# A two-block layer stack on one core: where remainders of weights are made, 512-column products in the second block, and the order of opening, norms and closing

## The chip, the cores and the metric

The kernel runs on one core of one Trainium2 chip. The metric is the device time of one execution in microseconds (us); lower is better. A core has TensorE (PE, the matrix engine; its weight loads are shown apart as PEld), VectorE (DVE), ScalarE (ACT), GpSimd (POOL) and SyncE (SP, which here only issues transfers). Each engine works through its own list of instructions in order and waits on semaphores of the others. All matrices are float32.

## The reference, cut to what matters

The input x is 256 tokens by 1024 features. Two blocks follow each other.

```python
# block 1
h = rms_norm(x, pre_mix_norm)
att_q, att_k, att_v, gdn_qkv, gdn_z, gdn_a, gdn_b = split(h @ w_in)
o_att = softmax attention, 8 heads of 64, causal, with a relative bias
o_gdn = gated delta rule: conv + silu, triangular solve per chunk, gated norm
x = x + rms_norm(concat(o_att, o_gdn) @ w_out, post_mix_norm)
h = rms_norm(x, pre_mlp_norm)
x = x + rms_norm(square(relu(h @ w_up)) @ w_down, post_mlp_norm)
# block 2
h = rmsnorm(x, g_mix)
xc, gb, gc, q, k, v, g_sw, gate_a, gate_r = split(h @ w_in_2)
y_a = (gb * conv3(gc * xc)) @ w_a_out_2          # 3 taps along the tokens
ret = two-way retention of rotary(q), rotary(k), v; 4 heads, decays from dec_f, dec_b
y_r = (normalized(ret) * silu(g_sw)) @ w_r_out_2
x = x + (sigmoid(gate_a) * y_a + sigmoid(gate_r) * y_r) @ w_o_2
h = rmsnorm(x, g_ffn)
x = x + (silu(h @ w_ff_gate_2) * (h @ w_ff_up_2)) @ w_ff_down_2
out = rmsnorm(x, g_final)
```

## The kernel before, in words

**Split products.** Every large product is made of three products of a 32-bit type that PE reads at full rate (fp32r). A value a is cut into a leading part ah (a cast) and a remainder al = a - ah, a weight w into wh and wl, and the product is wh*ah + wh*al + wl*ah.

**Units of weights.** The weights are streamed in 144 units of 1 MB (2048 numbers on each of 128 partitions; the first is half as large) in an order fixed by `plan()`. SP copies unit i into one of three slots of `raw`, once the remainder of unit i-3 is made. ACT makes the leading part `wh` (`hi`, line 1095), DVE the remainder `wl` (`lo`, line 1545), each in one of four slots. Both engines make unit i+2 where their list says `next_unit()` for unit i, between other work. PE may start a unit when its remainder is there. So a `lo` in DVE's list stands ahead of whatever comes behind it there, and each unit's arrival depends on where in the two lists `next_unit()` was written.

**Kinds of units.** `b_unit` (line 439) has the weights stationary and 256 tokens moving: 8 slices of k times 2 blocks of output columns times 3 products of 256 columns, all into one bank. `wide_unit` (lines 465 and 468) does the same unit with the leading part and the remainder of x side by side as one moving operand of 512 columns: 16 products of 512 columns with wh, 16 of 256 columns with wl, into two banks, whose right halves hold the sum of wh*al. Somebody must then add the halves: ACT copies the right halves out (line 1367 in the first MLP, 1512 and 1517 in the last) and DVE adds the left halves to the copy. `a_unit` (497) and `a_pair` (522) have activations stationary and 512 columns of weights moving, 24 products a unit. Only the two MLPs use `wide_unit`; the second block's 28 units for xc, gc, gb, the rotated q and k (`rot`) and g use `b_unit`.

**Banks.** The eight PSUM banks are 0 to 3, given out by name, and 4 to 7, given out in turn by `take`. `opened(b)` makes PE wait until the former content of bank b was read.

**Order of the stages** (us in the trace): opening, norm of x and transposes, 0 to 13; the projections of block 1 with the decay work, to 116; solving a triangular system in levels (line 728) with the eight heads of attention between its steps, to 154 (`att(n)` does the next n of 24 steps; `BESIDE` says how many go where); out projection with the delta rule's remaining small products (lines 779 to 866), to 200; `between("mlp")`, norms between mixer and MLP, to 215; first MLP, to 382; `between("mix2")`, to 397; in block 2 the groups i = 0..3 of xc, gc, gb with the convolution, to 467; rotations, `w_a_out`, scores and g, to 547; retention heads with g, gates and output products, to 750; the last MLP, to 935; closing norm, to 942.

**between.** DVE multiplies the product of token half t with its norm weights out of PSUM (`products`), ACT sums its squares, POOL takes the root (line 2130), DVE adds it to x (`post_half`), ACT sums the squares of x (`norm_x`), POOL again the root, both scale x (`scale_x`), PE transposes, ACT writes the leading parts (line 1145), DVE the remainders (line 1571), and PE runs two "C" units on them, once for each half t. The next unit's `hi` and `lo` come behind all that.

**The convolution's groups.** For each i, DVE makes uc = gc*xc, three taps for two halves, multiplies with gb, makes the remainder yl, and then two steps of the decay table `Dm` for head i. ACT makes the leading part yh and the exponential of `Dm`, and only then the next group's first `hi`; DVE's next `lo` waits for that.

## Time and profile before

| | us |
|---|---|
| median of 3 runs | 939.38 |
| the three runs | 939.35, 939.38, 943.61 |
| the profiled execution: its time | 943.77 |
| the profiled execution: first to last instruction | 942.0 |

| engine | busy, share of the span |
|---|---|
| PE | 97% |
| PEld | 85% |
| DVE | 62% |
| ACT | 47% |
| POOL | 9% |

The profiled execution's 943.77 us are its span of 942.0 and 1.8 us around it. The engines' rows tell when each was busy; what counts is what PE waited for, and at which clock it ran. The chain of waits is the list of what released what, followed back from the last instruction.

### The profile page before, as it was taken

What the parts mean: (1) busy time and instruction counts of PE and PEld (TensorE: products, weight loads), DVE (VectorE), ACT (ScalarE), POOL (GpSimd) and SP (SyncE); (2) the same over time, 40 slices, a digit from 0 to 9 for tenths busy, and PEclk for the clock granted to TensorE, in tenths of its full rate; (3) what the DMA queues carried; (4) which work ended last, traced back from release to release, by engine and by line L of the source; (5) the groups of instructions that cost most, each with busy time, mean ns of one, the idle gap of its engine ahead of it and who ended that gap; (6) DMA issues with size and microseconds to landing.
All of it is one profiled execution on the core that took longest, in us unless ns stands there. A gap on an engine that the chain in (4) does not pass through costs nothing.

```text
span 942.0 us, 13539 instructions
## 1 busy us (share of the span) xinstructions
PE 915.6 (97%) x5876; PEld 797.1 (85%) x5876; DVE 584.6 (62%) x671; ACT 446.5 (47%) x528; POOL 85.2 (9%) x92
## 2 busy tenths in 40 slices
PE   6999998999999999999999999999999999999996
PEld 5988887878888888799989988887888888888885
DVE  5689955467556656658674655545457657565554
ACT  5765364265444445654344244443444565454442
POOL 2033010010000000100032230101100000000000
PEclk9999997799999999999999999999999999999999
DMA  8635413215544455365564534454544445546431
GB/s 307 240 134 180 143 44 112 90 46 200 224 180 179 181 201 206 108 232 222 181 224 136 177 114 159 180 205 147 179 180 178 179 148 192 219 178 220 175 142 46
DMA packets 24220, 159.86 MB, mean 170 GB/s; under 512 B 3240, under 2 KB 3512, under 8 KB 5856
## 3 DMA queue, kind: packets, MB, share of 16 engines
q1 hardware_dynamic: 21600, 152.58, 44.5%
q0 software_dynamic: 2272, 6.24, 1.9%
q8 instruction: 46, 0.75, 0.3%
q10 hardware_dynamic: 288, 0.17, 0.1%
q14 instruction: 14, 0.11, 0.0%
HBM read 157.91 MB, written 2.63 MB: 170 GB/s over the span
## 4 chain that ended last, share of the span: by engine, by line
PE 87%; DVE 6%; ACT 4%; issue 2%; DMA 0%; POOL 0%; DVEq 0%; POOLq 0%; ACTq 0%
PE banks L497 32%; PE banks L439 22%; PE banks L465 13%; PE banks L468 7%; PE banks L522 3%; DVE t_wl L1545 2%; PE banks L418 2%; PE banks L728 2%; PE banks L975 1%; ACT t_wh L1095 1%; ACT t_hold L1114 1%; ACT t_hx L1145 1%; PE banks L926 1%; PE banks L1057 1%; DVE t_hx L1571 1%
## 5 line engine op out<-in xcount | busy, mean ns | idle before, releaser
L1545 DVE TENSOR_TENSOR t_wl<-t_raw,t_wh 128x2048 fp32r<-128x2048 f32 (+1 forms) x143 | 325.2, 2297 | 142.1 <-ACT t_wh L1095 140.5
L1095 ACT CAST t_wh<-t_raw 128x2048 fp32r<-128x2048 f32 (+1 forms) x143 | 267.0, 1898 | 35.3 <-PE banks L439 20.0
L439 PE MATMUL banks<-t_hx,t_wh 128*128 128x256 f32 x1232 | 225.2, 285 | 0.4 <-DVE t_wl L1545 0.4
L439 PEld LDWEIGHTS banks<-t_hx,t_wh 128*128 128x128 f32 x1232 | 193.8, 193 | 2.5 <-DVE t_wl L1545 0.8
L439 PE MATMUL banks<-t_hx,t_wl 128*128 128x256 f32 x616 | 175.0, 284 | 0.0
L465 PE MATMUL banks<-t_hx,t_wh 128*128 128x512 f32 x544 | 170.9, 396 | 0.4 <-DVE t_wl L1545 0.4
L468 PEld LDWEIGHTS banks<-t_hx,t_wl 128*128 128x128 f32 x544 | 102.2, 188 | 23.9
L439 PEld LDWEIGHTS banks<-t_hx,t_wl 128*128 128x128 f32 x616 | 119.0, 193 | 0.0
L468 PE MATMUL banks<-t_hx,t_wl 128*128 128x256 f32 x544 | 107.0, 278 | 0.0
L497 PE MATMUL banks<-t_wh,t_hx 128*128 128x512 f32 x320 | 103.9, 402 | 0.0
L465 PEld LDWEIGHTS banks<-t_hx,t_wh 128*128 128x128 f32 x544 | 84.5, 189 | 2.6 <-DVE t_wl L1545 0.8
L497 PEld LDWEIGHTS banks<-t_wh,t_hx 128*128 128x128 f32 x320 | 60.5, 191 | 13.1 <-issue 0.3
L497 PE MATMUL banks<-t_wl,t_hx 128*128 128x512 f32 x160 | 61.9, 396 | 0.0
L2130 POOL TENSOR_TENSOR t_st<-t_st,t_half 128x1 f32<-128x1 f32 (+1 forms) x18 | 10.6, 589 | 443.0 <-DVE t_st L1571 434.8
L497 PEld LDWEIGHTS banks<-t_wl,t_hx 128*128 128x128 f32 x160 | 30.6, 192 | 6.5 <-issue 0.2
L1367 ACT COPY t_tail<-banks 128x512 f32<-128x512 f32 x14 | 8.2, 586 | 57.8 <-PE banks L468 57.8
L497 PE MATMUL banks<-t_wh,t_mh 128*128 128x512 f32 x112 | 34.6, 390 | 0.0
L497 PE MATMUL banks<-t_wl,t_mh 128*128 128x512 f32 x112 | 34.5, 389 | 0.0
L497 PE MATMUL banks<-t_wh,t_ml 128*128 128x512 f32 x112 | 34.5, 389 | 0.0
L1563 DVE TENSOR_TENSOR t_rl<-banks,t_tail 128x512 f32<-128x512 f32 x14 | 9.7, 691 | 30.5 <-ACT t_tail L1367 30.4
L2225 POOL TENSOR_SCALAR t_gt<-t_gt,t_small 128x256 f32<-128x256 f32 x16 | 14.9, 942 | 111.7 <-ACT t_gt L1456 111.7
L497 PEld LDWEIGHTS banks<-t_wl,t_mh 128*128 128x128 f32 x112 | 21.0, 188 | 4.5
(296 smaller groups left out, 1217.1 us busy)
## 6 DMA issues: line engine op xcount, KB each, us to landing
t_raw<-in_W SPq DMA_DIRECT2D x143, 1024.0 KB, 4.9
skew<-scr POOLq DMA_DIRECT2D x1, 1536.0 KB, 17.2
t_x<-in_x SPq DMA_DIRECT2D x2, 512.0 KB, 4.8
t_T<-skew POOLq DMA_DIRECT2D x8, 128.0 KB, 2.4
out<-t_xt SPq DMA_DIRECT2D x4, 256.0 KB, 2.1
t_tab<-in_tab POOLq DMA_DIRECT2D x1, 640.0 KB, 6.1
t_raw<-in_W SPq DMA_DIRECT2D x1, 512.0 KB, 6.6
t_T<-skew POOLq DMA_DIRECT2D x8, 64.0 KB, 2.6
```

Source lines behind the costliest of these rows:

```text
L418: return e.transpose(o, i, ident[:])
L439: m = e.matmul(bank[b][:, c * S:c * S + S], W[w][:, h, k * 128 * nt + c * 128:k * 128 * nt + c * 128 + 128], H[a][:, k, :], start=first, s ...
L465: e.matmul(bank[b + c], M.wh[:, h, wk], M.hx[:, k, :, :].rearrange("p a s -> p (a s)"), start=k == 0, stop=False)
L468: m = e.matmul(bank[b + c][:, 0:S], M.wl[:, h, wk], M.hh[:, k, :], start=False, stop=k == 7)
L497: m = e.matmul(bank[outs[t][c]][:], act[a][:, ks[kk], t * 128:t * 128 + 128], W[w][:, h, kk * 512 * ncb + c * 512:kk * 512 * ncb + c * 512 ...
L522: m = e.matmul(bank[outs[t][c]][:], act[a][:, k, t * 128:t * 128 + 128], W[w][:, (i0 + u) % HR, kk * 1024 + c * 512:kk * 1024 + c * 512 + ...
L728: m = e.matmul(bank[b][p, i * 64:i * 64 + 64], left(p), right(p), start=True, stop=True)
L1095: e.copy(M.wh[:, h, 0:n], M.raw[:, r, 0:n]).then_inc(q.sem, q.tick(("hi", i)))
L1545: e.tensor_tensor(M.wl[:, h, 0:n], M.raw[:, r, 0:n], M.wh[:, h, 0:n].bitcast(F32), ALU.subtract).then_inc(q.sem, q.tick(("lo", i)))
L1563: return e.tensor_tensor(o, a, b, op).then_inc(q.sem, q.tick(*names))
L2130: return e.tensor_tensor(o, a, b, op).then_inc(q.sem, q.tick(*names))
L2225: e.tensor_scalar(M.gt[:, a, :], M.gt[:, a, :], gw[:, 4 * h + a:4 * h + a + 1], None, ALU.mult).then_inc(q.sem, q.tick(("gt", h, a)))
```

## The change

It does six things.

1. In attention, DVE's `next_unit()` that stood behind level 2's steps (a `lo`, line 1545) stands between the two groups of steps of level 1.
2. The 28 `b_unit`s of block 2 become `wide_unit`s. ACT copies the right halves into one of two slots of `M.rest` (`rest`), DVE adds the left halves (`whole`), and what read the bank reads the sum. gc and gb use banks 0 to 3; of the rotations, `rotate(h, 1)` goes ahead of `scores(h - 1)`.
3. The opening: PE starts with 14 products of `M.half` that nobody reads; the bias product goes to bank 0; unit 1 is made in halves (`hi_halves`, `lo_half`), and its product runs with k outside and starts at the first half.
4. `between`: the squares of half 1's first product are summed ahead of half 0's scaling, `post_half` and the sums of x's squares of half 1 go between the parts of half 0, and the unit that follows is made in halves.
5. The eight numbers of `log_decays` are made during the first MLP.
6. The closing multiplies x with g_final ahead of the root, and DVE scales 640 and ACT 384 columns with it.

```diff
--- before.py
+++ after.py
@@ -263,6 +263,7 @@
+    M.rest = M.wbc.rearrange("p (i n) -> p i n", i=2)
@@ -417,19 +418,21 @@
-            def b_unit(tile, arrived, by, name, kind="B", k_outer=False, mid=None):
+            def b_unit(tile, arrived, by, name, kind="B", k_outer=False, mid=None, halved=False):
...
-                q.wait_ge(DV, ("lo", i))
+                q.wait_ge(DV, ("lo", i, 0) if halved else ("lo", i))
...
+                    if k == 4 and halved:
+                        q.wait_ge(DV, ("lo", i))
...
@@ -584,8 +589,13 @@
+            q.wait_ge(PO, "half")
+            for i in range(14):
+                e.matmul(bank[7][:, 0:128], M.half[:], M.half[:], start=True, stop=True)
...
-            b = take("bias")
+            b = take("bias", 0)
@@ -609,7 +619,8 @@
-                b_unit(("conv", u), x_in, AC, ("cin", u), mid=queries_and_keys if u == 5 else None)
+                b_unit(("conv", u), x_in, AC, ("cin", u), k_outer=u == 0, halved=u == 0,
+                       mid=queries_and_keys if u == 5 else None)
@@ -909,15 +920,15 @@
-                b_unit(("xc", i), x_mix2, AC, ("gcv", i), k_outer=i == 0)
-                b_unit(("gc", i), x_mix2, DV, ("uc", i))
-                b_unit(("gb", i), x_mix2, DV, ("cvg", i))
+                wide_unit(("xc", i), x_mix2, DV, ("gcv", i))
+                wide_unit(("gc", i), x_mix2, DV, ("gcs0", i), pair=0)
+                wide_unit(("gb", i), x_mix2, DV, ("gbs0", i), pair=2)
...
-                b_unit(("rot", h, w), x_mix2, DV, ("rb", h, w))
+                wide_unit(("rot", h, w), x_mix2, DV, ("turned0", h, w))
...
-                b = take(("sc", h))
+                b = take(("sc", h), h)
@@ -930,9 +941,9 @@
+                rotate(h, 1)
...
-                rotate(h, 1)
...
@@ -964,9 +976,9 @@
-                    if h or u:
-                        b_unit(("g", h, u), x_mix2, AC, ("gts", h, u))
-                bs = [take(("rv", h, n)) for n in range(2)]
+                    if h:
+                        wide_unit(("g", h, u), x_mix2, DV, ("gsm", h, u))
+                bs = [take(("rv", h, n), None if h else n) for n in range(2)]
...
@@ -1148,22 +1161,25 @@
-                    if t:
+                    if (t, c) == (1, 1):
...
+                norm_x(g, 0)
+                squares(1, 0)
...
-                    norm_x(g, t)
...
-                        if t == 0 and k in (2, 4):
-                            squares(1, k // 2 - 1)
+                        if t == 0 and k == 2:
+                            squares(1, 1)
+                        if t == 0 and k >= 6:
+                            norm_half(g, 1, k - 6)
...
-                    if t == 1:
-                        hi(unit[0] + 3)
-                        unit[0] += 2
+                hi_halves()
+                hi(unit[0] + 3)
+                unit[0] += 2
@@ -1177,6 +1193,7 @@
+            hi_halves()
@@ -1382,6 +1399,11 @@
+                if i == 9:
+                    q.wait_ge(DV, "sp0")
+                    e.activation(M.sp, M.sp, ACT.Exp).then_inc(q.sem, q.tick("sp1"))
+                    q.wait_ge(q, "sp1")
+                    e.activation(M.sp, M.sp, ACT.Ln, bias=1.0).then_inc(q.sem, q.tick("sp2"))
@@ -1391,30 +1413,34 @@
...
+            rests = [0]
...
+            def rest(tile, seen):
...
+                s = rests[0] % 2
+                rests[0] += 1
+                q.wait_ge(PE, tile)
+                if seen:
+                    q.wait_ge(DV, seen)
+                e.copy(halves(M.rest[:, s, :]), both(M.banks, at[tile], 1)).then_inc(q.sem, q.tick((tile, "rest")))
...
-                q.wait_ge(PE, ("xc", i))
-                if i >= 2:
-                    q.wait_ge(DV, ("cyl", i - 2))
-                e.copy(M.gcv[:, i % 2], halves(bank[at["xc", i]][:])).then_inc(q.sem, q.tick(("gcv", i)))
-                next_unit()
-                next_unit()
+                rest(("xc", i), ("gcs", i - 1) if i else None)
+                next_unit()
+                rest(("gc", i), ("gbs", i - 1) if i else None)
+                next_unit()
+                rest(("gb", i), ("gcv", i))
...
-                if i == 0:
-                    log_decays()
...
-                next_unit()
+                rest(("rot", h, 0), ("turned", h - 1, 0) if h else ("gcs", 3))
+                next_unit()
+                rest(("rot", h, 1), ("turned", h - 1, 1) if h else ("gbs", 3))
...
@@ -1448,13 +1475,12 @@
-                    if h or u:
+                    if h:
...
-                    q.wait_ge(PE, ("g", h, u))
-                    if h:
-                        q.wait_ge(DV, ("rlo", h - 1, 1))
-                    e.activation(M.gt[:, 2 * u:2 * u + 2, :], halves(bank[at["g", h, u]][:]), ACT.Silu).then_inc(
-                        q.sem, q.tick(("gts", h, u)))
+                    rest(("g", h, u), ("gsm", h - 1, u) if h else ("turned", 3, u))
+                    gated = M.gt[:, 2 * u:2 * u + 2, :]
+                    q.wait_ge(DV, ("gsm", h, u))
+                    e.activation(gated, gated, ACT.Silu).then_inc(q.sem, q.tick(("gts", h, u)))
@@ -1526,6 +1552,10 @@
+                q.wait_ge(DV, ("xg", t, 0))
+                q.wait_ge(PO, ("rstd", "out", t))
+                e.activation(M.xt[:, t, 0:384], M.xt[:, t, 0:384], ACT.Copy, scale=M.ms[:, t:t + 1]).then_inc(
+                    q.sem, q.tick(("out", t)))
...
@@ -1612,29 +1642,34 @@
-            def post_half(g, t):
...
+            def post_half(g, t, c):
...
-                for t in range(2):
-                    post_half(g, t)
-                    norm_x(g, t)
-                    scale_x(g, t)
-                    if t == 0:
-                        products(g, 1, arrived)
-                        trailing_of_x(g, 0, range(0, 5), w)
-                        mean_square(g, 1)
-                        trailing_of_x(g, 0, range(5, 8), w)
-                    else:
-                        trailing_of_x(g, 1, range(8), w)
-                        lo(unit[0] + 3)
-                        unit[0] += 2
+                post_half(g, 0, 0)
+                post_half(g, 0, 1)
+                norm_x(g, 0)
+                scale_x(g, 0)
+                products(g, 1, arrived)
+                trailing_of_x(g, 0, range(0, 2), w)
+                mean_square(g, 1)
+                trailing_of_x(g, 0, range(2, 4), w)
+                post_half(g, 1, 0)
+                trailing_of_x(g, 0, range(4, 5), w)
+                post_half(g, 1, 1)
+                trailing_of_x(g, 0, range(5, 8), w)
+                norm_x(g, 1)
+                scale_x(g, 1)
+                trailing_of_x(g, 1, range(8), w)
+                lo_half(0)
+                lo_half(1)
+                lo(unit[0] + 3)
+                unit[0] += 2
@@ -1649,6 +1684,8 @@
+            lo_half(0)
+            lo_half(1)
@@ -1809,9 +1846,10 @@
-                att(sum(BESIDE[l]))
-                if l == 2:
+                att(BESIDE[l][0])
+                if l == 1:
...
+                att(BESIDE[l][1])
...
@@ -1902,6 +1941,15 @@
+                if i == 8:
+                    ts(M.lg, dec, -1.0, None, ALU.mult, None, "lg0")
+                    q.wait_ge(q, "lg0")
+                    stt(M.sp, M.lg, -1.0, M.lg, ALU.mult, ALU.min, "sp0")
+                elif i == 10:
+                    q.wait_ge(AC, "sp2")
+                    stt(M.sp, M.lg, 0.0, M.sp, ALU.max, ALU.add, "sp3")
+                    q.wait_ge(q, "sp3")
+                    ts(M.lg, M.sp, -1.0, None, ALU.mult, None, "lg")
@@ -1912,24 +1960,25 @@
...
+            rests = [0]
...
+            def whole(o, tile, name):
...
+                s = rests[0] % 2
+                rests[0] += 1
+                q.wait_ge(AC, (tile, "rest"))
+                tt(o, both(M.banks, at[tile], 0), halves(M.rest[:, s, :]), ALU.add, name)
...
-                next_unit()
-                q.wait_ge(PE, ("gc", i))
-                q.wait_ge(AC, ("gcv", i))
+                whole(M.gcv[:, s], ("xc", i), ("gcv", i))
+                next_unit()
+                v = halves(M.rest[:, rests[0] % 2, :])
+                whole(v, ("gc", i), ("gcs0", i))
+                q.wait_ge(q, ("gcs0", i))
...
-                tt(M.uc[:, s, :, 1:S + 1], halves(bank[at["gc", i]][:]), M.gcv[:, s], ALU.mult, ("uc", i))
+                tt(M.uc[:, s, :, 1:S + 1], v, M.gcv[:, s], ALU.mult, ("uc", i), ("gcs", i))
@@ -1943,14 +1992,14 @@
-                q.wait_ge(PE, ("gb", i))
+                v = halves(M.rest[:, rests[0] % 2, :])
+                whole(v, ("gb", i), ("gbs0", i))
+                q.wait_ge(q, ("gbs0", i))
...
-                tt(M.cv[:, s], M.cv[:, s], halves(bank[at["gb", i]][:]), ALU.mult, ("cvg", i))
+                tt(M.cv[:, s], M.cv[:, s], v, ALU.mult, ("cvg", i), ("gbs", i))
...
-                if i == 0:
-                    log_decays()
@@ -1959,15 +2008,16 @@
-                v = halves(bank[at["rot", h, w]][:])
-                q.wait_ge(PE, ("rot", h, w))
+                v = halves(M.rest[:, rests[0] % 2, :])
+                whole(v, ("rot", h, w), ("turned0", h, w))
+                q.wait_ge(q, ("turned0", h, w))
...
-                tt(halves(M.ra[:, w, 1, :]), v, rep(M.rope[:, 1, :], 2), ALU.mult, ("rb", h, w))
+                tt(halves(M.ra[:, w, 1, :]), v, rep(M.rope[:, 1, :], 2), ALU.mult, ("rb", h, w), ("turned", h, w))
...
@@ -2113,13 +2165,17 @@
-                add_back("out", "ff", t)
+                for c in range(2):
+                    d = M.x[:, t, cols(c)]
+                    q.wait_ge(PE, ("ff", t, c))
+                    tt(d, d, bank[2 * t + c][:], ALU.add, ("add", "out", t, c))
+                    q.wait_dma(LD["g_final"])
+                    q.wait_ge(q, ("add", "out", t, c))
+                    tt(M.xt[:, t, cols(c)], d, M.wbc[:, cols(c)], ALU.mult, ("xg", t, c))
...
-                for c in range(2):
-                    q.wait_ge(PO, ("rstd", "out", t))
-                    q.wait_dma(LD["g_final"])
-                    stt(M.xt[:, t, cols(c)], M.x[:, t, cols(c)], M.ms[:, t:t + 1], M.wbc[:, cols(c)], ALU.mult,
-                        ALU.mult, ("out", t, c))
+                q.wait_ge(PO, ("rstd", "out", t))
+                q.wait_ge(q, ("xg", t, 1))
+                ts(M.xt[:, t, 384:1024], M.xt[:, t, 384:1024], M.ms[:, t:t + 1], None, ALU.mult, None, ("out", t))
...
```

## Rows read from the trace of the kernel before

**Rows 1.** The page: busy us, share, instructions; granted clock in 40 slices, in tenths
```profile
PE 915.6 (97%) x5876; PEld 797.1 (85%) x5876; DVE 584.6 (62%) x671; ACT 446.5 (47%) x528; POOL 85.2 (9%) x92
...
PEclk9999997799999999999999999999999999999999
```
**Rows 2.** Windows: stretch, length, busy of PE, PEld, DVE, ACT, POOL, granted clock, DMA
```profile
14.00:16.00 2.00, 2.00 (x11) 2.00 (x11) 2.00 (x5) 2.00 (x2) 0.37 (x1) 0.50 1.02 431
...
149.80:152.50 2.70, 0.01 (x1) 0.01 (x1) 2.60 (x4) 0.58 (x1) 0.00 (x0) 1.00 0.00 0
...
153.85:174.33 20.48, 20.48 (x138) 17.10 (x140) 10.11 (x14) 5.35 (x6) 2.20 (x2) 0.50 0.46 170
```
**Rows 3.** The chain of waits, 149 to 178: start, us, what
```profile
149.58 2.20 DVE t_wl L1545
...
153.84 1.85 PE banks L789 x16
...
159.05 2.86 PE banks L497 x6
...
166.57 3.61 PE banks L840 x32
...
177.68 1.07 PE banks L789 x16
```
**Rows 4.** Timeline of attention: start, us, engine, line, operation [idle before]
```profile
138.67 0.56 DVE L1563 TENSOR_TENSOR t_P<-banks,t_T 128x384 f32<-128x384 f32 x1 [2.07 <-PE banks L660]
...
151.89 0.55 DVE L1567 TENSOR_SCALAR t_P<-t_P,t_gs 128x128 f32<-128x128 f32 x2
```
**Rows 5.** The chain of waits: first MLP, and block 2's units
```profile
233.05 5.45 PE banks L497 x24
244.06 5.45 PE banks L497 x24
...
507.50 11.51 PE banks L439 x96
```
**Rows 6.** DVE's timeline in the convolution's last group
```profile
466.75 0.69 DVE L1563 TENSOR_TENSOR t_cv<-t_cv,banks 128x512 f32<-128x512 f32 x1 [0.63 <-PE banks L439]
468.12 0.69 DVE L1563 TENSOR_TENSOR t_yl<-t_cv,t_yh 128x512 fp32r<-128x512 f32 x1 [0.69 <-ACT t_yh L1409]
...
472.56 2.29 DVE L1545 TENSOR_TENSOR t_wl<-t_raw,t_wh 128x2048 fp32r<-128x2048 f32 x1 [2.56 <-ACT t_wh L1095]
```
**Rows 7.** Windows: the convolution's last group, from one such lo to the next
```profile
455.28:472.56 17.28, 17.28 (x147) 17.28 (x146) 12.21 (x14) 7.30 (x7) 0.00 (x0) 1.00 0.51 183
```
**Rows 8.** Timeline of the first MLP: the copy of the right halves and the sum
```profile
244.10 0.59 ACT L1367 COPY t_tail<-banks 128x512 f32<-128x512 f32 x1 [4.62 <-PE banks L468]
...
244.78 0.69 DVE L1563 TENSOR_TENSOR t_rl<-banks,t_tail 128x512 f32<-128x512 f32 x1 [2.53 <-ACT t_tail L1367]
```
**Rows 9.** Timeline between the blocks
```profile
386.19 1.41 DVE L1571 SCALAR_TENSOR_TENSOR t_x<-t_xt,t_st,t_x 128x512 f32<-128x512 f32 x2
389.36 0.49 DVE L1567 TENSOR_SCALAR t_xt<-t_x,t_st 128x512 f32<-128x512 f32 x1 [0.66 <-POOL t_st L2130]
...
394.99 4.49 DVE L1545 TENSOR_TENSOR t_wl<-t_raw,t_wh 128x2048 fp32r<-128x2048 f32 x2 [1.51 <-ACT t_wh L1095]
...
397.34 0.50 PE L439 MATMUL banks<-t_hx,t_wh 128*128 128x256 f32 x2 [0.42 <-DVE t_wl L1545]
```
**Rows 10.** Timeline of the opening
```profile
11.66 3.22 DVE L1571 SCALAR_TENSOR_TENSOR t_hx<-banks,t_small,t_hx 128x256 fp32r<-128x256 f32 x8
...
12.59 0.81 PE L592 MATMUL banks<-t_cout 32*8 32x384 f32 x2 [1.63 <-DVE t_hx L1571]
...
15.27 4.47 DVE L1545 TENSOR_TENSOR t_wl<-t_raw,t_wh 128x2048 fp32r<-128x2048 f32 x2
```
**Rows 11.** Timeline of the closing
```profile
935.80 0.69 DVE L1563 TENSOR_TENSOR t_x<-t_x,banks 128x512 f32<-128x512 f32 x1 [0.67 <-PE banks L522]
...
938.09 1.41 DVE L1571 SCALAR_TENSOR_TENSOR t_xt<-t_x,t_st,t_hold 128x512 f32<-128x512 f32 x2 [0.66 <-POOL t_st L2130]
```

55 lines of the change are left out of this document (23 added, 32 removed).

## The prediction, made before the changed kernel ran

> **What bounds the kernel now.** I read the page's busy times first: PE is busy 97% of the span and no other engine over 62% [rows 1]. So time can go only where PE is idle, where it runs on a low clock, or where its own products get cheaper. The windows come next, for the granted clock. It is full nearly everywhere, but from 153.85 to 174.33 us it is 0.50 (1.2 instead of 2.4 GHz) while PE is busy for all 20.48 us, and it is 0.50 once more behind the opening [rows 2]. Ahead of the long stretch PE was idle for 2.70 us, from 149.80 to 152.50 [rows 2]. The chain of waits says why: DVE's remainder of a weight unit (line 1545) runs from 149.58 to 151.78, and behind it in DVE's list stands the norm of attention's last head, from 151.89, which PE's next transposes wait for [rows 3, 4]. The reader should see there that an instruction of 2.2 us which nobody needs at that moment stands between two that somebody waits for, and that the stretch at half clock begins right behind the idle it makes.
>
> **Attention (edit 1).** The idle goes from 2.70 us to about 0.5: once its last remainder of attention's output is made at 149.58, DVE goes straight to the norm, whose two scalings (0.55) and the small reciprocal ahead of them end at 150.25 [rows 3, 4]. That is 2.2 us. The moved remainder lands behind DVE's work for head 4 or so, at about 136.6, and ends at about 138.9. The addition that stands behind it starts at 138.67 today after an idle time of 2.07 us [rows 4], so it is late by some 0.2 us and PE's next transposes are a level further on: cost 0. If that cover were gone it would cost at most the 2.2 us again. The unit's slot of raw data comes free 13 us sooner, so one transfer moves to a time in which DMA was idle; no price.
>
> What follows if PE's idle stays at 0.5 us is the larger part. I expect the clock not to fall, since between the opening and 153.85 it stayed at 2.4 GHz [rows 1] through all of attention's shorter waits, and fell behind the one of 2.70. Then 20.48 us of busy PE run at twice the clock. Two kinds of work stand in the chain at either level: the 16 products of line 789 took 1.85 us at half and 1.07 at full clock, a factor of 1.73; six products of line 497 took 2.86 at half, and 24 take 5.45 at full, so six take 1.36, a factor of 2.1 [rows 3, 5]. The stretch therefore shrinks to between 9.8 and 11.8 us: a gain of 8.6 to 10.7. I take 9.8, as the line-840 products (3.61 us) [rows 3] and the other small ones lie between. What is late next: DVE's and ACT's copies of 0.6 to 0.7 us between the triangular solve's products, which half clock covered. I count 0.2 us for them, with 2 as the far end. Sum for attention: 2.2 + 9.8 - 0.2 = 11.8 us (range 7 to 12.9 with the clock up).
>
> **Wide units in block 2 (edit 2).** A `b_unit` takes 11.51/2 = 5.755 us, 48 products at 120 ns. In the first MLP one period is 244.06 - 233.05 = 11.01 us, of which 5.45 are the 24 products of line 497, so a `wide_unit` takes 5.56 [rows 5]. The 28 units save 28 x 0.19 = 5.4 us. The moving columns are the same in number: 512 + 256 against 3 x 256. What is saved is a fixed part of some 12 ns for each product left out. The Trainium skill (TensorE: Matmul & The Clock Gate, Back-to-back issue gap) gives an isolated gap of N/2.4 + 2.5 ns, by which one 512-column product instead of two of 256 saves 2.6 ns and the 28 units about 1.2 us as an estimate; the rows' 120 ns speak against it, and the sum goes by them.
>
> Each of these units now costs ACT a copy of 0.59 us and DVE a sum of 0.69 [rows 8], and 28 of each lie in engines that are not the bound. The exception is the convolution. There DVE, ACT and DVE form a ring: DVE's work of one group, then ACT's exponential and its cast of the next unit (DVE idle 2.56 us), then DVE again. One turn today is 12.21 us of DVE's work, 2.56 for that and 0.69 in which DVE waits for ACT's yh: 15.5 us [rows 6, 7], against PE's 3 x 5.755 = 17.3. The change adds 3 x 0.69 us and a few hundredths for each wait of DVE on itself: 17.6 to 17.8. PE's three units shrink to 16.7. So the ring, not PE, sets the pace at an excess of about 1 us a group. Its reserve: the remainder that starts at 472.56 is ready at 474.8, and its unit is due when PE has done two more units after the last gb, which ended by 466.7: at 478.2. That is 3.4 us, of which the copy and sum of gb take 1.3 and the shorter units 0.4, which leaves 1.7. Four turns use up 4 and PE waits about 2 us in all (0 to 4.5). log_decays' removal from the first group (edit 5) gives that turn some 2 us back, but the first turn has PE behind the norms anyway; I count 0, and 0 for its work in the first MLP, whose ACT and DVE are idle 4.6 and 2.5 us a unit there [rows 8]. The rotations, scores and g units have far less DVE work per unit; their longer path (copy, sum, then what read the bank) of 1.3 us is covered by at least one more unit of PE, 5.5 us. Cost 0; with the cover gone, 1.3 us for each of 16. Net of edits 2 and 5: 5.4 - 2.0 = 3.4 us (0.9 to 5.4).
>
> **Between (edit 4), twice.** Half 1's path today is: `post_half` begins at 386.19, its two parts of 0.7, ACT's two sums, the root, the scaling at 389.36, transposes, then ACT's cast and DVE's remainder from 394.99, and PE's next unit at 397.34, released by that remainder [rows 9]. With the parts set between half 0's remainders, the second addition ends about 0.9 us sooner, and the path is then held by ACT, which has two sums and two leading parts to do in turn: scaling at about 388.4. The cast and remainder in halves overlap: half a cast (1.0) and half a remainder (1.2) are no longer in line, so the unit is ready 0.8 us sooner again. PE's own "C" unit then ends at about the same moment (24 products, 5.45 us, after half 1's first remainder). I take 1.6 us for each `between`, 3.2 in all (2 to 4).
>
> **Opening (edit 3).** The first unit starts at 13.4 today, behind a bias product of 0.81 us that itself waited 1.63 us for a bank which DVE was reading [rows 10]. With bank 0 it waits for nothing and leaves the line. The first unit is then paced by DVE's eight remainders of x (3.22 us from 11.66, so up to 14.88) and ends at 15.3 to 16.5, by the clock. The next starts at 17.8 today; with `lo_half(0)` behind the remainders (14.9 + 1.2) it starts at 16.1 to 16.5. The half clock seen at 14 to 16 us [rows 2] may stay, and then takes some 0.5 back. I take 1.2 us (0.3 to 1.9). The 14 products that nobody reads run while PE has nothing else until 7.0; even at half clock they end about then: 0, or 0.3 against.
>
> **Closing (edit 6).** Behind the last root DVE has two products of 0.7 us, 1.41 from 938.09 [rows 11]. Now ACT and DVE each do one part at once, about 0.6 us, and the multiplication with g_final falls into DVE's idle time around 935.80. The last transfer starts 0.8 us sooner but is larger (320 KB against 256 KB) and runs beside the other. I take 0.5 (0 to 0.8).
>
> **Sum.** 11.8 + 3.4 + 3.2 + 1.2 + 0.5 = 20.1 us off the profiled execution's 943.8 (span 942.0 and 1.8 around it): 923.7 us. That execution is 4.4 us above the median; one of the three timed runs is as high (943.61), two are at 939.4. What differs between them isn't in one trace. The length of the stretch at half clock is the likeliest, and since that is to go, I measure from the profiled execution and expect 15.7 us (1.7%) against the median. If the 4.4 us are something else, the new median is 919.3.
>
> **Rivals.** First, the clock falls all the same. For it: attention's last steps and the solve are small products with small gaps, and it fell once in the opening with PE partly busy. Against: it held through 130 us of the same kind of work. Then only the idle of 2.2 us goes and the other edits' 8.3: 943.8 - 10.5 = 933.3 us. Second, the ring in the convolution and the longer path in the other groups cost more, 5 us beyond the sum: 928.7. Third, the 4.4 us lie elsewhere: 919.3. Fourth, slower: each time PE waits for the ring in the convolution the clock falls as it did behind the 2.70 us, and a stretch like the one seen (20.48 us, 9.8 lost) follows. It decides from two such falls on, which take back the whole gain against the median; with four groups and three falls it is 923.7 + 29 = 953. Against it: the expected waits are about 1 us each and waits of that size left the clock alone elsewhere. The Trainium skill (TensorE: Matmul & The Clock Gate, A second HAM failure mode: psum-queue depth-cycling) tells of a kernel of 512-column products in which short idle times between groups made the clock swing between its two levels; the first MLP, which has such products, shows no swing here, so I give the rival little. Fifth, the edits in attention don't shorten anything, since something else holds PE at 150 as long: 935.
>
> **How the numbers follow.** The forecast has a chance of 0.62, the first rival 0.12, the second 0.1, the third 0.1, slower 0.03, the fifth 0.03. The range from 918.0 to 931.5 us holds the forecast with its bounds, the second and the third; the first (933.3) is left out. Against 939.4, a difference under 0.5% (4.7 us) is about what a measurement of this kernel can't tell from none, so faster begins at 934.7: the forecast, the first three rivals but for some of the first, 0.92. Same, between 934.7 and 944.1: 0.05. Slower 0.03.
>
> **What would show it.** Right: no window of half clock near 150 to 175, PE's idle there under 1 us, the part from 149.8 to the out projection's last group 12 us shorter; the wide units at 5.56 us; waits of PE on line 1545 of 1 us each in the third or fourth group of the convolution; PE's first unit behind each `between` 1.6 us sooner. Wrong: a granted clock of 0.50 over ten or more us, PE idle on DVE or ACT in the rotations or in the heads, or a `between` as long as before because ACT's sums come later than the transposes.

## The result, and the profile after

The changed kernel takes 927.82 us (median of 4 executions, 924.72 to 928.88) against 939.37 for the kernel before beside it (938.82 to 943.61, 4 executions): ratio 0.986, 95% interval 0.983 to 0.990. The prediction was 923.7 us with a range of 918.0 to 931.5. So the direction was right and the time lies in the range, 4.1 us above the forecast: of the 15.7 us that were expected against the median of before, 11.6 were measured.

The page of the changed kernel shows what [rows 1] showed of before: busy us and share of each engine, then the granted clock in 40 slices.

```profile
PE 906.8 (98%) x5456; PEld 770.2 (83%) x5456; DVE 603.7 (65%) x704; ACT 461.4 (50%) x557; POOL 91.1 (10%) x92
...
PEclk9999999999999999999999999999999999999999
```

PE has 420 products fewer and is busy 8.8 us less, and the slices at 0.7 in attention are gone. The windows (length, busy time of PE, PEld, DVE, ACT and POOL, granted clock, DMA) answer to [rows 2]:

```profile
12.30:15.70 3.40, 3.18 (x15) 3.21 (x16) 3.40 (x8) 3.40 (x6) 0.00 (x0) 0.51 1.02 424
32.70:36.10 3.40, 3.40 (x19) 3.40 (x19) 2.42 (x2) 3.35 (x5) 0.14 (x1) 0.52 0.31 127
150.00:175.00 25.00, 24.07 (x262) 19.20 (x259) 14.50 (x20) 11.62 (x17) 2.21 (x2) 1.00 0.29 106
```

The long stretch at 1.2 GHz is gone. The one in the opening (12.30 to 15.70) is there still, and there is a second one behind it, which before did not have. The chain of waits of the changed kernel (start, length, what), cut to one line for each place that the change touches:

```profile
17.75 7.14 DMA scr<-t_cout
...
32.94 13.10 PE banks L442 x96
...
120.49 2.01 PE banks L739 x64
...
152.69 0.56 DVE t_P L1597 x2
...
153.30 0.55 PE banks L419 x3
...
180.27 4.10 PE banks L527 x18
...
387.23 0.70 PE banks L470 x2
...
465.86 22.08 PE banks L502 x96
```

Read against [rows 3]: the norm of the last head (DVE, two scalings, 0.56) and PE's transposes now follow one another with no remainder of 2.2 us ahead of them, and PE's wait for that norm (us in total, times, longest) is 0.5 where it was 2.7:

```profile
PE banks L419 <- DVE t_P L1597: 0.5, 1, 0.5
```

The opening, though, has a transfer in its chain for 7.14 us which in before was nowhere in the chain. Marks that both kernels pass at the same point of their work turn this into a table (start of the mark in us from the span's start, profiled executions; the last column is the difference that the part itself adds):

| mark | before | after | part | its share |
|---|---|---|---|---|
| first products of the triangular solve (x64) | 117.48 | 120.49 | opening, edit 3 | +3.0 |
| out projection's pair of units (x18) | 188.00 | 180.27 | attention, edit 1 | -10.7 |
| first MLP's first output products (x24) | 222.02 | 213.01 | first place between blocks, edit 4 | -1.3 |
| first MLP's last ones behind a wide unit (x24) | 354.19 | 345.18 | first MLP | 0.0 |
| first unit of block 2 | 397.34 | 387.23 | second place between blocks, edit 4 | -1.1 |
| products of `w_a_out` behind the convolution (x96) | 478.23 | 465.86 | convolution, edits 2 and 5 | -2.3 |
| first rv products (x8) | 552.97 | 539.42 | rotations and scores | -1.2 |
| last MLP, start | 751.41 | 736.69 | heads | -1.2 |
| last MLP, near its end | 907.17 | 892.42 | last MLP | 0.0 |
| end of the span | 942.0 | 927.1 | closing, edit 6 | -0.1 |

The sum is 14.9 us between two profiled executions, where 20.1 were forecast. The 5.2 missing are mostly the opening (+3.0 instead of -1.2), and attention, which gave 10.7 instead of 11.8. The profiled execution of the changed kernel (928.88) is the slowest of its four, 1.1 above their median, and the experiments show that its opening is the worst one seen. So this table explains the profiled execution; the opening of a median execution need not have lost as much.

### The profile page after: what moved, and what is told of

Read it like the earlier page. It is cut to its first block, busy times and chain, and to the rows that moved or that the text cites. A ratio compares the mean times of both kernels' runs of the same rounds, so it can differ in the third digit from the quotient of the medians.

```text
span 927.1 us, 12760 instructions
## 1 busy us (share of the span) xinstructions
PE 906.8 (98%) x5456; PEld 770.2 (83%) x5456; DVE 603.7 (65%) x704; ACT 461.4 (50%) x557; POOL 91.1 (10%) x92
## 4 chain that ended last, share of the span: by engine, by line
PE 79%; DVE 11%; ACT 6%; issue 2%; DMA 1%; POOL 1%; POOLq 0%; DVEq 0%; ACTq 0%
PE banks L502 32%; PE banks L470 20%; PE banks L473 10%; DVE t_wl L1575 4%; PE banks L442 4%; ACT t_wh L1107 2%; PE banks L527 2%; PE banks L739 2%; PE banks L419 2%; PE banks L987 1%; PE banks L582 1%; DMA scr<-t_cout 1%; DVE t_hx L1601 1%; PE banks L937 1%; PE banks L1069 1%
## 5 line engine op out<-in xcount | busy, mean ns | idle before, releaser
L1575 DVE TENSOR_TENSOR t_wl<-t_raw,t_wh 128x2048 fp32r<-128x2048 f32 (+1 forms) x140 | 319.2, 2302 | 125.9 <-ACT t_wh L1107 124.7
L470 PE MATMUL banks<-t_hx,t_wh 128*128 128x512 f32 x992 | 312.2, 396 | 1.0 <-ACT t_vv L1185 0.5
L1107 ACT CAST t_wh<-t_raw 128x2048 fp32r<-128x2048 f32 (+1 forms) x140 | 262.5, 1899 | 13.1 <-DMA t_raw<-in_W 7.6
L473 PE MATMUL banks<-t_hx,t_wl 128*128 128x256 f32 x992 | 194.9, 278 | 0.0
L470 PEld LDWEIGHTS banks<-t_hx,t_wh 128*128 128x128 f32 x992 | 153.2, 189 | 4.0 <-DVE t_wl L1589 1.8
L502 PE MATMUL banks<-t_wh,t_hx 128*128 128x512 f32 x320 | 102.0, 395 | 0.0
L442 PE MATMUL banks<-t_hx,t_wh 128*128 128x256 f32 x336 | 64.2, 293 | 1.5 <-DVE t_hx L1601 1.5
L442 PEld LDWEIGHTS banks<-t_hx,t_wh 128*128 128x128 f32 x336 | 54.8, 201 | 2.6 <-DVE t_hx L1601 2.2
L1425 ACT COPY t_hold<-banks 128x512 f32<-128x512 f32 x28 | 16.4, 585 | 68.6 <-PE banks L473 57.5
L442 PE MATMUL banks<-t_hx,t_wl 128*128 128x256 f32 x168 | 48.8, 290 | 0.0
```

Source lines behind the costliest of these rows:

```text
L442: m = e.matmul(bank[b][:, c * S:c * S + S], W[w][:, h, k * 128 * nt + c * 128:k * 128 * nt + c * 128 + 128], H[a][:, k, :], start=first, s ...
L470: e.matmul(bank[b + c], M.wh[:, h, wk], M.hx[:, k, :, :].rearrange("p a s -> p (a s)"), start=k == 0, stop=False)
L473: m = e.matmul(bank[b + c][:, 0:S], M.wl[:, h, wk], M.hh[:, k, :], start=False, stop=k == 7)
L502: m = e.matmul(bank[outs[t][c]][:], act[a][:, ks[kk], t * 128:t * 128 + 128], W[w][:, h, kk * 512 * ncb + c * 512:kk * 512 * ncb + c * 512 ...
L1107: e.copy(M.wh[:, h, 0:n], M.raw[:, r, 0:n]).then_inc(q.sem, q.tick(("hi", i)))
L1425: e.copy(halves(M.rest[:, s, :]), both(M.banks, at[tile], 1)).then_inc(q.sem, q.tick((tile, "rest")))
```

## Experiments

Three questions were open. Is the gain in attention the idle time or the clock, and does the one always cause the other? What does the opening lose, and where? What do wide units, their ring and the two places between the blocks cost by themselves? "Before beside it" is the kernel before on the same chip in the same session.

**The opening: bias row first.** DVE makes the relative bias row ahead of the halves of the first remainder, as before had it; all else is the changed kernel.

```diff
-            lo_half(0)
-            lo_half(1)
             q.wait_ge(PE, "bias")
             q.wait_dma(LD["neg"])
             tt(M.rrow, bank[at["bias"]][0:8, 0:384], M.ng, ALU.add, "row")
+            lo_half(0)
+            lo_half(1)
```

> Theory (transfer queued behind weights): in the changed kernel the 12 KB row for the attention bias is ready on DVE only after the two halves of the first remainders, its transfer is issued at 17.75 us, behind a weight transfer that the second half released at 16.9, and takes 7.1 us instead of 1.8; ACT's first tap and so PE's 'sums' product wait for it. Here DVE makes the row ahead of the two halves and nothing else is changed. The transfer should be issued at about 15.8, land by 18 us, PE's wait of 3.5 us on line 1601 should fall to the 0.5 of the kernel before, no window of half clock near 33 to 36 us: 3 to 5 us less than the changed kernel's 927.8, so 923 to 925, 0.982 to 0.985 of the kernel before. Rival (the opening is late for another reason, such as the 14 products or DVE's extra halves): the transfer lands early but the 3 us at 46 us stay: 927 to 928.

**The opening: nobody waits for the transfer.** The order of the changed kernel stays, but ACT waits for the row's transfer only from its third part on, and POOL clears the pad ahead of it.

```diff
-                q.wait_dma(LD["scr"])
+                if u == 2:
+                    q.wait_dma(LD["scr"])
...
+            e.memset(M.cin[:, :, 0:3], 0.0).then_inc(q.sem, q.tick("pad"))
             q.wait_ge(DV, "row")
...
-            e.memset(M.cin[:, :, 0:3], 0.0).then_inc(q.sem, q.tick("pad"))
```

> Same theory, from the other side: the order on DVE stays that of the changed kernel and the transfer stays slow, but nobody waits for it where it hurts. ACT waits for it only from the third convolution unit on (the first whose output lies over the row), and POOL clears the padding ahead of it. Expected as above: PE's wait of 3.5 us gone though the transfer still takes about 7 us, 923 to 925 us. If instead it is the place of the row among DVE's work that costs, this run stays at 927 to 928 and only the run with the row first is faster.

Measured: 926.21 us (926.01 to 928.09, 4 executions, ratio 0.984, 0.979 to 0.989) with the row first and 926.01 (924.44 to 928.18, ratio 0.984, 0.979 to 0.988) without the wait. Both were expected at 923 to 925 and missed that. They are 1.6 and 1.8 below the changed kernel's median, not the 4.3 that the opening of its profiled execution lost; in both profiles some of it went again in attention, where the clock fell near 160 us (table below). The DMA view from 12 to 30 us (out<-in, queue, operation, KB, median us from issue to landing) of the kernel before, of the changed one, and of the one with the row first:

```profile
scr<-t_cout POOLq DMA_DIRECT2D x1, 12.0 KB, 1.8
```
```profile
scr<-t_cout POOLq DMA_DIRECT2D x1, 12.0 KB, 7.1
```
```profile
scr<-t_cout POOLq DMA_DIRECT2D x1, 12.0 KB, 2.0
```

What waited for it, in the changed kernel: POOL's timeline, one line of ACT's, and the waits of PE (us in total, times, longest).

```profile
17.75 0.53 POOL L2216 DMA_DIRECT2D scr<-t_cout  x1 [8.53 <-DVE t_cout L1593]
25.16 1.11 POOL L2218 DMA_DIRECT2D skew<-scr  x1 [6.89 <-DMA scr<-t_cout]
26.26 0.15 POOL L2219 MEMSET t_cin<- 128x36 f32 x1
...
26.50 0.91 ACT L1233 ACTIVATE t_cout<-t_cin,t_small 128x256 f32<-128x256 f32 x2 [3.04 <-POOL t_cin L2219]
...
PE banks L636 <- DVE t_gs L1601: 3.5, 1, 3.5
```

With the row first that wait of PE is 0.5, and without ACT's wait it is 0.5 too:

```profile
PE banks L636 <- DVE t_gs L1601: 0.5, 1, 0.5
```

The first products of the solve come at 116.21 and 116.46 instead of 120.49. Both cures work, by separate ways, so the path is shown: the row was made 2.1 us later (16.91 instead of 14.80), its transfer of 12 KB started at 17.75 instead of 15.6, and there it took 7.1 us instead of 1.8. In the seven other profiles with the late start it took 4.3 to 6.2 us, in the six with the early start 1.8 to 2.0.

What lies between the two starts can be seen in the DMA's columns (the last two: busy share of the DMA engines, GB/s), first in before, then in the changed kernel:

```profile
17.00:18.00 1.00, 1.00 (x9) 1.00 (x9) 1.00 (x2) 0.00 (x0) 0.24 (x1) 0.84 0.00 0
```
```profile
18.00:24.89 6.89, 6.89 (x60) 6.89 (x59) 3.85 (x2) 1.90 (x2) 0.27 (x1) 1.00 0.96 356
```

In all profiles the engines are all but idle from 17 to 18 us, and then the next weights of 1024 KB come, which SP issued at 17.0 to 17.6. The early transfer lands ahead of them. The late one is issued behind them: in the changed kernel SP issues at 17.02, POOL at 17.75, and POOL's queue moves no packet before 21 us. Why it takes 7.1 us in one execution and 4.3 in another stays open.

How much this costs differs as much. In the six other profiles that have both the late row and ACT's wait for its transfer, PE waits 0.7 to 2.2 us instead of 3.5, and the solve's first products come at 116.52 to 118.50, against 116.21 with the row first and 117.48 in before. So the profiled execution of the changed kernel is the worst of seven: there the moved row cost 4.3 us, in the others 0.3 to 2.3, and in four of these six the opening is still 0.5 to 1.0 us shorter than in before. PE's wait of 3.5 us is also followed by the second stretch at half clock (32.7 to 36.1), which no profile with a wait of 2.2 us or less shows there. With the row first the opening gains 1.3 us over before, where 1.2 were forecast.

**Attention alone.** The kernel before with edit 1 and nothing else:

```diff
-                att(sum(BESIDE[l]))
-                if l == 2:
+                att(BESIDE[l][0])
+                if l == 1:
                     next_unit()
+                att(BESIDE[l][1])
```

> The kernel before with edit 1 alone (DVE's remainder moved between the steps of attention's level 1). Theory: PE's idle of 2.7 us ahead of the last head's transposes goes to 0.5 and the stretch at half clock behind it goes too; in the profile, 10 to 12 us less between 145 and 175 us than in the kernel before. Against the median of the kernel before 7 to 11 us less (928 to 932), depending on how long that kernel's typical stretch at half clock is. Rival (the clock falls for another reason, such as the small products themselves): a stretch at 0.50 in this profile too, and only 2.2 us less, 937.

**The kernel before again**, unchanged, for a second profile:

> The kernel before unchanged, for a second look. Theory for the 4.4 us between its executions: a fast execution (939.4) has a shorter stretch at half clock behind 150 us than the 20.5 us of the one profiled, by some 8 to 9 us, or starts its opening differently. If this profile falls at 943 too, its stretch should be about as long as the first. Rival: a time of 939 with the same 20.5 us at half clock, and the difference elsewhere.

**Attention undone.** The changed kernel with that edit taken back, the same lines the other way round:

> The changed kernel with edit 1 undone, in three rounds. Theory: PE's idle of 2.7 us is back, 2.2 us are always lost, and in some executions the clock falls behind it for long, as in the kernel before, whose 14 executions lie at 937 to 939 and at 944 to 945 us. So two groups of times here too: about 928 to 930, and 934 to 937. Rival (the long fall comes from the kernel's other small products and not from this idle time): all executions within 2 us of the changed kernel's 927.8 + 2.2.

Measured: attention alone 935.01 us (934.32 to 936.30, 10 executions) against a median of 943.5 for before beside it (936.77 to 944.99, 13 executions), ratio 0.993 (0.991 to 0.996). Before again 936.88. Attention undone 931.93 (931.06 to 936.66, 10 executions), ratio 0.993 (0.990 to 0.996). Attention alone missed its 928 to 932; between profiles the part from the solve to the out projection got 9.3 us shorter (70.5 to 61.2), where 10 to 12 were expected. Attention undone has two groups, as expected, the lower one 1 to 2 us later than expected. The second profile of the kernel before is the telling one. Its chain, and its windows at the place where [rows 2] had 0.50:

```profile
151.22 2.20 DVE t_wl L1545
...
154.14 0.55 PE banks L418 x3
...
149.50:154.10 4.60, 1.94 (x37) 1.47 (x36) 3.25 (x5) 1.55 (x4) 0.00 (x0) 1.00 0.00 0
153.80:174.30 20.50, 19.73 (x200) 15.86 (x201) 12.86 (x18) 8.62 (x9) 2.20 (x2) 1.00 0.54 181
```

The same remainder of 2.20 us stands in the same place, PE is idle for the same 2.7 us (4.60 less 1.94), and the clock does not fall. In the changed kernel with edit 1 undone it does fall, for as long as in [rows 2]:

```profile
153.40:173.90 20.50, 20.50 (x140) 17.11 (x141) 10.25 (x14) 5.29 (x6) 2.20 (x2) 0.50 0.47 169
```

and with edit 1 alone there is a short fall further on, behind PE's waits at the end of the solve:

```profile
161.10:164.50 3.40, 3.40 (x18) 2.30 (x17) 1.76 (x5) 0.00 (x0) 1.51 (x1) 0.50 0.97 330
```

From the solve's first products (x64) to the out projection's pair (x18), with attention's last heads between, the profiles give, by PE's idle time ahead of the last head and by the time at half clock from 150 to 175 us:

| kernel profiled | idle, us | half clock, us | length, us |
|---|---|---|---|
| before | 2.7 | 20.5 | 70.5 |
| attention undone | 2.7 | 20.5 | 70.5 |
| before again | 2.7 | 0 | 62.0 |
| no wait for the transfer | 0.5 | 6.8 | 62.9 |
| attention alone, row first, narrow units | 0.5 | 3.4 | 61.2, 61.3, 61.3 |
| after, and three variants of it | 0.5 | 0 | 59.8, each |
| remainder later | none to 0.5 | 0 | 59.2 |

That splits the gain of 10.7 without a model: 62.0 - 59.8 = 2.2 us are the idle time; 70.5 - 62.0 = 8.5 us are the clock, which go only where it falls for as long. And it shows that the fall isn't settled by the kernel: with the same idle time one execution has it and another has not. The times of the kernel before say the same. Of its 48 executions beside the experiments 30 took 935.0 to 939.6 us and 18 took 943.5 to 945.1, with nothing between; the upper ones have a mean clock of 0.986 to 0.988, the lower ones 0.992 to 0.998. With edit 1 alone ten of ten lie under 936.4. With edit 1 undone four of ten lie at 936.2 to 936.7 and six at 931.1 to 932.3. So edit 1 takes away the upper group, and taking edit 1 back brings it again: that the long fall hangs on the remainder's place, and the idle time that it makes, is shown both ways.

The distance between the groups' medians is 5.8 us (944.6 and 938.8), though, and not 8.5. The second profile of before, at 936.88, is one of the six fastest of the 30 (up to 936.9, mean clock 0.996 to 0.998); the other 24 take 937.5 to 939.6 at 0.992 to 0.995. So the usual executions of before show more time at half clock than those six, and with edit 1 undone the lower six, at 0.991 to 0.992, more still. None of these was profiled, and where their clock falls is not shown; part of it can lie in the opening. It fits that attention alone is 3.8 us under the median of the lower group, more than the 2.2 of the idle time.

The Trainium skill (TensorE: Matmul & The Clock Gate, What's actually happening) says that half rate is the default state which activity lifts, and that the moment at which the chip judges activity isn't tied to the start of the kernel, so that executions of one kernel differ. The traces agree: here one and the same 2.7 us of idle time was followed by a fall that cost 8.5 us in two profiles, and by none in a third.

**Narrow units.** The changed kernel with edits 2 and 5 undone: block 2 in `b_unit`s of three times 256 columns.

```diff
-                wide_unit(("xc", i), x_mix2, DV, ("gcv", i))
-                wide_unit(("gc", i), x_mix2, DV, ("gcs0", i), pair=0)
-                wide_unit(("gb", i), x_mix2, DV, ("gbs0", i), pair=2)
+                b_unit(("xc", i), x_mix2, AC, ("gcv", i), k_outer=i == 0)
+                b_unit(("gc", i), x_mix2, DV, ("uc", i))
+                b_unit(("gb", i), x_mix2, DV, ("cvg", i))
```

> The changed kernel with edits 2 and 5 undone: block 2's 28 units are narrow again (three products of 256 columns) and the decays' logarithms are made in the convolution. Read by stage in the trace: from the first unit behind the second 'between' to the first w_a_out unit 80.9 us as in the kernel before (78.6 in the changed one), and to the last MLP's first line-502 unit 4.6 us more than the changed kernel. Rival (the gain of block 2 came from the moved logarithms or from less waiting, not from the width): the 14 units of the convolution and first rotations take under 80 us here too.

**The ring.** The changed kernel, with ACT's cast of the next unit ahead of its copy of `gb` and of the exponential's part behind it:

```diff
                 next_unit()
+                hi(unit[0] + AHEAD)
                 rest(("gb", i), ("gcv", i))
```

> The changed kernel, with ACT's cast for the next group's third unit ahead made while PE still works on gb, so that DVE's next remainder no longer waits for ACT's exponential and cast. Theory (the ring of DVE and ACT sets the pace of the convolution's groups, 17.3 us a turn against 16.7 of PE): DVE's idle of 2.56 us ahead of that remainder vanishes, and the stretch from the first wide unit to w_a_out falls from 78.6 to 77.9 us, no more, since PE's reserve had covered nearly all of the ring. Rival (the ring had cost the 2 us that were forecast): 76.6 or less.

Measured: narrow 931.14 us, ring 924.44 (one execution each). From block 2's "C" units to the end of the span, narrow units take 557.6 us (371.80 to 929.4), the changed kernel 553.0 (374.12 to 927.1), the ring's variant 552.3 (370.33 to 922.6). So edits 2 and 5 gain 4.6 us, and 5.3 with the ring loosened; without any ring 5.4 were forecast. The rival of the narrow kernel (the gain came from the moved logarithms or from less waiting) is out: its 14 units take 80.86 us, as before had it (80.89), with the changed kernel's 78.63 beside them:

```profile
384.91 80.86 PE banks L441 x672
```

The chain of the changed kernel shows the ring at work, one remainder of DVE to the next of the following group:

```profile
402.92 2.20 DVE t_wl L1575
...
420.23 2.20 DVE t_wl L1575
...
437.55 2.20 DVE t_wl L1575
...
454.86 2.20 DVE t_wl L1575
```

One turn is 17.3 us, not the 17.6 to 17.8 of the forecast. The windows of the third turn, to set beside [rows 7]:

```profile
437.55:454.86 17.31, 17.31 (x101) 15.09 (x100) 13.92 (x18) 8.75 (x9) 0.00 (x0) 1.00 0.52 184
```

DVE is busy for 13.92 us of it, 1.71 more than in [rows 7], where three sums of 0.69 had been forecast as 2.07. PE's idle time from it is one wait at the end of the convolution, in the waits of PE:

```profile
PE banks L502 <- DVE t_wl L1575: 0.3, 1, 0.3
```

With the ring's cast moved that line is gone, the convolution is 0.4 us shorter, and the output products behind it (x96) take 21.79 instead of 22.08. The ring cost 0.7 us where 2.0 were forecast, 0.4 of it in the convolution itself, where 0.7 had been expected.

**Copies first, between the blocks.** In both places ACT's two copies that empty the first units' banks go ahead of its cast of the next unit.

```diff
-                hi(unit[0] + 3)
-                unit[0] += 2
                 for t in range(2):
                     q.wait_ge(PE, ("first", g, t))
                     e.copy(dst[:, t, :], bank[at["first", g, t]][:]).then_inc(q.sem, q.tick(taken(t)))
+                hi(unit[0] + 3)
+                unit[0] += 2
```

> The changed kernel with ACT's two copies of the 'C' units' products ahead of the cast of the unit after the next, in both stretches between the blocks. Theory (with the bias product off the rotation of the banks, the first wide unit gets the bank of the first 'C' product, which ACT reads only behind a cast of 1.8 us): PE's two waits of 0.5 us on line 1185 go, each wide unit starts 0.5 us sooner, 1.0 us in all by stage. Rival (PE then waits for the remainder, line 1589, instead): under 0.3 us in all.

Measured: 926.69 us (one execution). The changed kernel has two waits that before did not have, one in each place:

```profile
PE banks L470 <- ACT t_vv L1185: 0.5, 1, 0.5
PE banks L470 <- ACT t_up L1185: 0.5, 1, 0.5
```

Both are gone with the copies first, but in the first place another one comes for them:

```profile
PE banks L502 <- DVE t_ml L1593: 1.3, 1, 1.3
```

There ACT's cast, now later, holds DVE's remainder, and behind that in DVE's list stands the first MLP's square. From the first place's "C" unit to the second's it takes 181.8 us instead of 180.9 (190.69 to 372.53, 193.22 to 374.12); from there to the output products behind the convolution 91.1 instead of 91.7. So the order gains 0.6 in the second place and loses 0.9 in the first, where 1.0 in all was expected.

**No warm products.** The changed kernel without the 14 products that nobody reads.

```diff
-            q.wait_ge(PO, "half")
-            for i in range(14):
-                e.matmul(bank[7][:, 0:128], M.half[:], M.half[:], start=True, stop=True)
```

> The changed kernel without the 14 products that nobody reads. Theory (they gain nothing, since the first units wait for x and for DVE): the first unit of the convolution ends within 0.3 us of the changed kernel's, the transposes take longer but end before anyone waits for them, and one stretch of half clock lies in the first 20 us as before. Rival (they hold the clock up): transposes at twice the length and the first two units 1 us or more later.

Measured: 924.87 us (one execution). The granted clock of that kernel reads 1.00 in the opening:

```profile
12.00:16.00 4.00, 3.97 (x18) 3.32 (x17) 4.00 (x10) 4.00 (x7) 0.00 (x0) 1.00 1.02 424
```

But the products don't bear that out. PE's timeline has the first eight transposes and two pairs of the first unit's products, all of one shape; below them are the transposes of the changed kernel:

```profile
7.07 1.97 PE L419 MATMUL banks<-t_ident,t_xt 128*128 128x128 f32 x8 [7.07 <-DVE t_xt L1594]
...
15.40 0.62 PE L442 MATMUL banks<-t_hx,t_wh 128*128 128x256 f32 x2
...
15.98 0.40 PE L442 MATMUL banks<-t_hx,t_wh 128*128 128x256 f32 x2
```
```profile
6.88 1.09 PE L419 MATMUL banks<-t_ident,t_xt 128*128 128x128 f32 x8 [0.34 <-DVE t_xt L1597]
```

A pair takes 0.62 us up to 15.8, as the pairs at a granted clock of 0.50 do in before (0.63), and 0.40 behind it. So here PE worked at half clock from its first product until 15.8 us, and the value of 1.00 ahead of that doesn't tell its clock. The second profile of before is another such case: its pairs take 0.63 until 19.6 us, at a shown clock of 1.00. Read by their products, all 14 profiles have half clock in the first unit of weights. It ends at 15.8 to 18.7 us in the ten with the 14 products and at 15.9, 17.3, 17.7 and 19.8 in the four without.

So the 14 products did raise the clock for the transposes (1.09 us instead of 1.97), but it fell again at 11.5 to 14.2 us, ahead of the first unit or in its first products, and the first unit started only 0.2 us sooner (12.52 instead of 12.71). Without them the solve's first products come at 116.52, no later than in any of the six profiles that differ in that (116.68 to 120.49 with the same late row and wait). They gained nothing that can be seen here, as expected.

**Remainder later.** In the changed kernel DVE's remainder of the next unit, which stood between two of attention's last steps (160.28 in the chain), goes behind the delta rule's residual `r1` (t_cin), which PE waits for.

```diff
-            next_unit()
             att(len(STEPS) - taken[0])
...
                     tt(M.r1, M.tm[:, 1, 1024:1536], M.r1, ALU.subtract, "r1")
+            next_unit()
```

> The changed kernel with DVE's next remainder moved behind the copies of the state's products. In the changed kernel and in two of its variants PE waits 0.42 us at about 159 to 163 us for a copy that stands behind that remainder (2.3 us) on DVE, and in three of four profiles a stretch of 3.4 to 6.8 us at half clock begins there. Theory (that wait starts the fall): the wait goes, no stretch at 0.50 near 160, 0.4 us plus up to 3 us less, 924 to 927. Rival (the products there are sparse enough to let the clock fall with no wait at all): the wait is gone and the stretch is there in some executions; the times spread over 3 us as before.

Measured: 925.75 us (925.13 to 926.50, 4 executions), ratio 0.984 (0.979 to 0.989). The part from the solve's first products to the out projection's pair takes 59.2 us instead of 59.8, the wait of 0.4 on that step is gone, and the clock is whole, here and in the two kernels below that have this edit too; of the eight profiles with edit 1 and the step in its old place, all with PE's wait of 0.4, four show a fall near 160. Three profiles without it agree with the theory that the wait starts it, and don't prove it:

```profile
150.00:175.00 25.00, 24.50 (x252) 19.91 (x248) 15.29 (x21) 10.52 (x13) 2.21 (x2) 1.00 0.36 126
```

**All of them.** Row first, no wait for the transfer, ring, copies first and remainder later:

> The changed kernel with the repairs together: the bias row made first and not waited for by the first convolution units, the early cast in the convolution's groups, the copies between the blocks ahead of the next cast, DVE's remainder behind the state's copies. By what each was seen to move in its own stage: about 3 us in the opening against the slowest and 0.5 against the usual executions, 0.7 in the convolution, 1 in the two stretches between the blocks, 0.4 and the falls near 160 us in attention. 921.5 to 923.5 us with a spread of under 2 us, against 924.7 to 928.9 for the changed kernel. Rival (they cover each other, or the clock falls elsewhere instead): no lower than 924.

**Copies first in the second place only**, and the rest as in the last one:

```diff
+                if g == "mlp":
+                    hi(unit[0] + 3)
+                    unit[0] += 2
                 for t in range(2):
...
+                if g == "mix2":
+                    hi(unit[0] + 3)
+                    unit[0] += 2
```

> The kernel before this one (c1_all, 923.86 us) had ACT's two copies of the first products' banks ahead of the next unit's leading part in both places between the blocks. In b3_copy_first that order gained 0.64 us in the second place (from the C units at 372.53 to attention's output at 463.63 it took 91.10 us instead of 91.74) but lost 0.94 in the first (190.69 to 372.53: 181.84 instead of 180.90), where DVE's t_ml and the output products behind it then come 1.3 us late. Here the copies go first in the second place only. Theory: the loss was that wait in the first place alone. Then 190 to 371 takes 180.9 again, PE waits 0.5 us on ACT's t_up there and not at all on t_ml, the stretch behind it keeps its 0.64, and the time is 922.9 us (922.3 to 924). Rival: the two orders are tied together through the ring of weight slots, so that the second place loses its gain when the first is put back: 923.6. Against the kernel before: 939 to 940, ratio 0.982.

Measured: 923.86 us (923.24 to 924.93, 6 executions), ratio 0.982 (0.978 to 0.985), and 923.75 (922.73 to 924.06, 6 executions), ratio 0.983 (0.980 to 0.986). In the profile of the last one the stretch from the first "C" unit to the second place's is 180.9 us and the next 90.6, the best of both, as the theory had it; the rival (the second place loses its gain) is out. The time as a whole did not follow: 0.1 us instead of 0.9. Its windows tell why, those of all together first and those of the last kernel second:

```profile
12.00:25.00 13.00, 12.36 (x91) 12.39 (x92) 10.79 (x16) 8.67 (x12) 1.63 (x2) 0.87 0.84 304
```
```profile
12.00:25.00 13.00, 12.43 (x81) 12.46 (x82) 9.99 (x13) 7.87 (x11) 1.63 (x2) 0.74 0.85 311
```

The last one's opening had 6.8 us at half clock instead of 3.4, and the solve's first products came 1.2 us later (117.50 instead of 116.29). For the one profiled execution that accounts for the gain; for the medians it remains argued. The first of the two missed its 921.5 to 923.5 narrowly, the second lies in its 922.3 to 924. Both kernels are some 4 us faster than the changed one, measured in other sessions, and 15 faster than the kernel before beside them.

## Why the prediction was right, and where it was not

The mechanisms of attention and of the wide units held, and with them the direction and most of the gain. That the time lies only 4.1 us from the forecast is in part luck: the wide units gave 1.3 more than forecast, and how far the opening goes wrong depends on the execution. No experiment tests the closing.

**Attention, 11.8 forecast, 10.7 measured.** The idle time was right to the tenth (2.2). The clock's part was 8.5 instead of the 9.6 left of 9.8 less 0.2. Both bounds of the step [rows 3, 5] came from products in a dense stream, where half clock costs a factor of 1.73 to 2.1. At full clock PE also waits there for copies of DVE and ACT, which the prediction priced at 0.2 us; in before again it was busy for only 19.73 of 20.50 us, 0.8 idle. That term was mis-sized. The sentence "the clock fell behind the wait of 2.70" took one execution for a rule: the idle time makes a fall possible, and the fall comes or does not.

**Where to measure from.** The prediction laid the 4.4 us between the profiled execution and the median to the stretch at half clock, and expected the changed kernel's median to equal its profile. The first is borne out for the upper group, which edit 1 takes away. The second is not: the median is 1.1 under the profile, and the usual execution of before, 4 to 5 us under its profiled one, has less to gain from the clock. The third rival (the 4.4 us lie elsewhere, 919.3) would need a gain of 20.1 in the median and didn't come. The first rival (the clock falls all the same) came in a small form that wasn't foreseen, 3.4 to 6.8 us near 160 in four profiles of kernels with edit 1, at a price of 1.5 to 3.1 us; the fifth (attention isn't shortened) is refuted.

**Opening, -1.2 forecast, +3.0 in the profiled execution and -1.0 to +1.0 in six other profiles: the step that failed.** The forecast followed PE and DVE's remainders, and left out the one row that edit 3 moves behind them, the bias row. From it hang POOL's transfer, POOL's clearing of the pad behind it in POOL's list, ACT's first tap, and PE's wait. The row of 0.54 us is in no term of the sum. Put back ahead, the opening gives 1.3 us, so the terms that were counted were sized well.

**Wide units, -3.4 forecast, -4.6 measured.** The saving of 5.4 stands (5.3 with the ring loosened), by the rows' 120 ns. The same runs refute the estimate of 1.2 us from the Trainium skill (TensorE: Matmul & The Clock Gate, Back-to-back issue gap); by that formula it should have read 2.5 ns a product and 1.1 us. The ring is the chain, as said, but its turn is 17.3 us instead of 17.6 to 17.8: the three sums add 1.71 us to DVE's busy time and not 2.07, and nothing came on top of that. With 17.3 the forecast's own working (four turns against PE's 16.7, less the reserve of 1.7) gives 0.7, which is what was measured. PE's expected waits of 1 us each didn't come, there is one of 0.3. The second rival (5 us more from the ring) and the fourth (clock falls at each wait of the ring, slower) fall with that: the convolution has no stretch at half clock in any profile.

**Between the blocks, -3.2 forecast, -2.4 measured.** The opening's bias product has left the rotation of the banks, so each first wide unit now takes a bank that ACT empties behind a cast of 1.8 us. That wait of 0.5 us in each place was not in the sum: banks were followed by their use and not by their numbers.

**Closing, -0.5 forecast, -0.1 measured.** From the last addition's start to the last scaling's end it takes 2.9 us instead of the 3.7 of [rows 11], the 0.8 of the forecast; the last transfers, 320 KB and 192 KB, end 3.1 us behind it instead of 2.5. That takes back 0.6 of the 0.8.
